# A one-core hybrid layer: the experts' first u and v are loaded and split during the gate stage, row sums come one step later, and adds of y move behind other readers of PSUM

## The chip, the cores and the metric

The kernel runs on one core of a Trainium2 chip. The metric is the device time of one execution in microseconds; the median of three runs of the kernel before is 3334.67 us (3320.79 to 3336.86).

## What is computed

One layer: a mixer (three kinds of attention on 1,024 tokens of 1,024 features), then PEER, a layer of 16,384 one-neuron experts. The last part is what the change touches, cut to its core:

```
q = (hb @ w_q).reshape(T, 8, 2, 128)                       # 8 heads, two half queries
s = einsum('thpd,pkd->thpk', q, keys)                      # 128 keys a half
top_s, top_i = top_k(s, 16); best_s, pos = top_k(all 256 sums of the two halves, 16)
idx = key_a * 128 + key_b of the best 16;  g = softmax(best_s)
act = gelu(einsum('thkd,td->thk', u[idx], hb))             # 128 experts a token
y   = einsum('thkd->td', g * act * v[idx])
out = x + gate2 * y
```

All is float32. Large products are done as three products of high and low parts (hi*hi, hi*lo, lo*hi).

## The kernel before, in words

After the mixer come three blocks: `route`, `gate_matrix` and `experts`. The 1,024 tokens are two halves. For the first 512 (tiles 0 to 3, "A") the chosen rows are gathered; for the second 512 (tiles 4 to 7, "B") all experts are computed densely.

- **Dots of A, ahead.** `Ahead` (L1366) computes the activations gelu(u x) of all 128 chunks of 128 experts for the A tokens while `route` and `gate_matrix` run: a chunk of u (512 KB) is loaded by SP, ScalarE makes its high part (`split_high`), GpSimd the low part (`split_low`), TensorE does 24 matmuls (`dots`), ScalarE the gelu, and SP stores the result to `act_scratch` in DRAM.
- **Gates of B.** `gate_matrix` builds for the B tokens the dense matrix of gates from one-hot products and stores it in 8 pieces of 4,096 KB to `gate_scratch`, issued by ScalarE. Its SP block ends by waiting for all stores; then the next block begins on all engines.
- **Experts.** `experts` (L1905) runs 64 steps of two chunks c = 0, 1 of 128 experts. In each, for the B tokens: u of the chunk is split into high (ScalarE) and low (VectorE), TensorE does 24 matmuls for the dots in PSUM (`dot_products`), ScalarE the gelu, VectorE multiplies with the gates (`weigh`) and makes the low part of the weights (`low_weights`), and in the next step TensorE multiplies the weights with v (`outputs`, 24 matmuls per c). Half of the outputs stays in PSUM over all steps (`held`), the other half (`y`) is added to `total` in SBUF by VectorE each step (`add`, four a step).
- **Rows of A.** Beside this GpSimd issues 16 indirect DMAs a step: 8 elements (`element`, L2009: the activation of one pick per token of a tile) and 8 rows (`row`, L2014: 128 rows of v, 512 KB, to one of 8 slots of `ring`). VectorE weights the picks (`weigh_picks`) and adds each row times its weight to `total` (`add_row`, L2152). GpSimd fetches a row for step s+1 once the row of step s has left the slot (`row_added`).

Each engine works through its instructions in the written order, so the place of each in VectorE's list is what decides. For one c of a step the order before is:

```
add_row(s, 4 * c, opening)
low_v(s, b, c)
add_row(s, 4 * c + 1, opening)
weigh(s, c)
low_u(n + 2, c, False)
low_weights(s, b, c)
add(s - 1, 2 * c, first)
add_row(s, 4 * c + 2, opening)
add_row(s, 4 * c + 3, opening)
add(s - 1, 2 * c + 1, first)
```

After 64 steps VectorE adds the last y, multiplies each of the 8 token tiles with `gate2` and adds x1 (`finish`), and SP stores it.

Of the kernel before, what the change touches and what calls it, by code (L numbers as in the profile page):

```python
# [13 lines left out]
F32 = mybir.dt.float32  # L14
F32R = mybir.dt.float32r
# [1350 lines left out]
class Ahead:  # L1366
# [3 lines left out]
    def __init__(self, nc, ctx, d, hi, lo, acts, tag, base):  # L1370
        sb, ps, sem = allocators(nc, ctx)
        self.nc, self.src, self.hi, self.lo, self.acts, self.base = nc, d["peer_u"], hi, lo, acts, base
        self.u = sb(tag + "u", [P, 2, KD, P])
        self.uhi = sb(tag + "uhi", [P, 2, KD, P], F32R)
        self.ulo = sb(tag + "ulo", [P, 2, KD, P], F32R)
# [63 lines left out]

class RouteInputs:  # L1440
# [14 lines left out]
def route(nc, k, d, hi, lo, first_T, second_T, gate_T, sparse, acts, inputs):  # L1455
# [9 lines left out]
    with ExitStack() as ctx:  # L1465
        sb, ps, sem = allocators(nc, ctx)
        first_key, second_key, gate = (sb(n, [P, NT, P]) for n in ("first_key", "second_key", "pick_gate"))
        ahead = Ahead(nc, ctx, d, hi[0], lo[0], acts, "ra_", 0)
# [298 lines left out]
def gate_matrix(nc, d, hi, lo, first_T, second_T, gate_T, scratch, acts):  # L1767
# [3 lines left out]
    with ExitStack() as ctx:  # L1771
        sb, ps, sem = allocators(nc, ctx)
        ahead = Ahead(nc, ctx, d, hi, lo, acts, "ga_", ROUTED)
# [10 lines left out]
        assert STEPS == NB // 2  # L1784

# [10 lines left out]
        with nc.Block() as block:  # L1796
            @block.sync
            def _(sp):
# [47 lines left out]
            def _(act):  # L1846
# [26 lines left out]
                block_pair(STEPS - 1, False, True)  # L1873

            @block.vector
            def _(dve):
# [21 lines left out]
                with dve.Fori(1, STEPS) as step:  # L1898
                    block_pair(step, False)

# [4 lines left out]
def experts(nc, k, d, hi, lo, total, scratch, acts, sparse, x1, result):  # L1905
# [10 lines left out]
    with ExitStack() as ctx:  # L1916
        sb, ps, sem = allocators(nc, ctx)
        u = sb("ex_u", [P, 2, KD, P])
        uhi = sb("ex_uhi", [P, 2, KD, P], F32R)
        ulo = sb("ex_ulo", [P, 2, KD, P], F32R)  # L1920
        v = sb("ex_v", [P, 2, D])
# [10 lines left out]
        u_in, v_in, g_in, pick_in = ([sem(f"ex_{n}_in{c}") for c in range(2)] for n in ("u", "v", "g", "pick"))  # L1932
# [3 lines left out]
        uhi_ready, ulo_ready, vhi_ready, vlo_ready, dots_ready, gelu_ready, weighted, whi_ready, wlo_ready, \  # L1936
            y_ready, y_added, held_ready, zeroed, pick_weighted, row_added = map(sem, (
                "ex_uhi_ready", "ex_ulo_ready", "ex_vhi_ready", "ex_vlo_ready", "ex_dots_ready",
# [6 lines left out]

        def one(a, n, pattern):
            return a[n] if isinstance(n, int) else a[bass.ds(n, 1)].rearrange(pattern)
# [12 lines left out]
        with nc.Block() as block:  # L1960
            @block.sync
            def _(sp):
                def load_u(n, c):
# [385 lines left out]
```

## Time and profile before

| | |
|---|---|
| median of the runs | 3334.67 us (3320.79 to 3336.86) |
| the profiled execution: own time / span | 3342.92 / 3341.1 us |
| TensorE busy | 3136.2 us (94%) |
| VectorE busy | 2363.6 us (71%) |
| GpSimd (POOL) busy | 1673.7 us (50%) |
| ScalarE busy | 1015.7 us (30%) |
| mean granted clock of TensorE | 0.963 of full speed |
| DMA | 645.75 MB, 193 GB/s over the span |

How to read it: the span is from the first to the last instruction of the profiled execution. Busy times of POOL include its indirect DMA issues, those of the other engines exclude their DMA issues. In the rows below PE is TensorE, DVE VectorE, ACT ScalarE, SP the engine that issues most loads; a row names the line of the kernel, the operation and its tiles (output <- inputs). Two operations in a row on one engine overlap by some 0.08 us in the rows, so the distance of two starts is the duration that counts. Up to 1836 us the mixer, routing and gate stages run, after it the expert stage.

### The profile page before, as it was taken

The page shows a single profiled execution, that of the slowest core. Times are in us where ns is not written, and L with a number is a line of the kernel's source. Part 1 is how long each engine was busy: PE and PEld are TensorE (multiplying, and loading weights), DVE is VectorE, ACT ScalarE, POOL GpSimd, SP SyncE. Part 2 cuts the span into 40 slices and gives each one's busy share as a digit, 9 for nine tenths or more (in the row PEclk, how much of TensorE's full clock was granted, in tenths as well). Part 3 has the DMA queues.
Part 4 walks back from the last instruction along what each step waited for, and adds up shares of the span by engine and source line. Part 5 has one row for each costly group of instructions (what it writes and reads, how often), then busy time and mean ns, then how long its engine had stood idle before and what let it go on. Part 6 is the DMA issues. An engine that isn't in the chain of part 4 may idle for free. (4 is left out here: it accounts for less than half of the span.)

```text
span 3341.1 us, 44529 instructions
## 1 busy us (share of the span) xinstructions
PE 3136.2 (94%) x14956; PEld 2541.8 (76%) x14956; DVE 2363.6 (71%) x4287; ACT 1015.7 (30%) x1182; POOL 1673.7 (50%) x1329
## 2 busy tenths in 40 slices
PE   6999588997999999999998799999999999999997
PEld 3889465686888887888887677777777877777776
DVE  4612465463688888666664688888888888888888
ACT  2110134432333323444444222222222222222221
POOL 2000224413433323333332777777777777777774
PEclk7999678998999999999999899999999999999999
DMA  5610000022332323445444898898898999999897
GB/s 208 212 64 26 10 14 26 1 91 91 111 107 88 107 79 123 159 160 214 163 163 189 272 298 298 288 297 287 293 299 302 304 301 300 298 306 300 292 306 283
DMA packets 325786, 645.75 MB, mean 193 GB/s; under 512 B 169264, under 2 KB 170560, under 8 KB 322752
## 3 DMA queue, kind: packets, MB, share of 16 engines
q1 hardware_dynamic: 233280, 338.08, 31.7%
q0 software_dynamic: 91264, 272.96, 23.1%
q10 hardware_dynamic: 1152, 33.55, 2.4%
q8 instruction: 51, 0.84, 0.1%
q14 instruction: 39, 0.32, 0.0%
HBM read 568.98 MB, written 75.50 MB: 193 GB/s over the span
## 5 line engine op out<-in xcount | busy, mean ns | idle before, releaser
L2152 DVE SCALAR_TENSOR_TENSOR total<-ex_ring,ex_pick,total 128x1024 f32<-128x1024 f32 x512 | 650.7, 1291 | 225.9 <-DMA ex_ring<-peer_v_dram,sp_row 217.6
L2009 POOL DMA_INDIRECT ex_pick<-act_scratch,sp_place x512 | 576.7, 1126 | 175.7 <-issue 155.7
L2014 POOL DMA_INDIRECT ex_ring<-peer_v_dram,sp_row x512 | 578.1, 1129 | 156.1 <-issue 129.9
L2042 PE MATMUL ex_dots<-h_hi_b,ex_uhi 128*128 128x512 f32 x1024 | 401.3, 392 | 23.7 <-ACT ex_uhi L2084 14.4
L2042 PE MATMUL ex_dots<-h_lo_b,ex_uhi 128*128 128x512 f32 x1024 | 400.7, 391 | 0.0
L1891 DVE TENSOR_SCALAR gm_b_hot<-gm_iota,second_T,gate_T 128x128 f32<-128x128 f32 x512 | 257.7, 571 | 170.1 <-PE gm_prod L1835 167.4
L2101 ACT ACTIVATE ex_whi<-ex_dots 128x512 fp32r<-128x512 f32 x128 | 76.8, 600 | 925.0 <-DVE ex_dots L2132 925.0
L1415 POOL TENSOR_TENSOR ga_ulo<-ga_u,ga_uhi 128x1024 fp32r<-128x1024 f32 x72 | 173.2, 2407 | 341.8 <-ACT ga_uhi L1409 341.6
L2045 PE MATMUL ex_dots<-h_hi_b,ex_ulo 128*128 128x512 f32 x1024 | 252.8, 389 | 0.0
L2052 PE MATMUL ex_y<-ex_vhi,ex_whi 128*128 128x512 f32 x512 | 216.3, 422 | 33.7 <-DVE total L2123 27.9
L2042 PEld LDWEIGHTS ex_dots<-h_hi_b,ex_uhi 128*128 128x128 f32 x1024 | 193.9, 189 | 64.9 <-ACT ex_uhi L2084 14.9
L1415 POOL TENSOR_TENSOR ra_ulo<-ra_u,ra_uhi 128x1024 fp32r<-128x1024 f32 x56 | 139.1, 2485 | 205.6 <-ACT ra_uhi L1409 205.6
L1425 PE MATMUL ga_dots<-h_hi_a,ga_uhi 128*128 128x512 f32 x576 | 229.9, 399 | 0.0
L2042 PEld LDWEIGHTS ex_dots<-h_lo_b,ex_uhi 128*128 128x128 f32 x1024 | 193.8, 189 | 40.3
L1425 PE MATMUL ga_dots<-h_lo_a,ga_uhi 128*128 128x512 f32 x576 | 224.5, 390 | 0.0
L2045 PEld LDWEIGHTS ex_dots<-h_hi_b,ex_ulo 128*128 128x128 f32 x1024 | 192.2, 188 | 39.9
L2052 PE MATMUL ex_y<-ex_vlo,ex_whi 128*128 128x512 f32 x512 | 201.1, 393 | 0.0
L2052 PE MATMUL ex_y<-ex_vhi,ex_wlo 128*128 128x512 f32 x512 | 200.8, 392 | 0.0
L2052 PE MATMUL ex_held<-ex_vhi,ex_whi 128*128 128x512 f32 x512 | 200.0, 391 | 0.0
L2052 PE MATMUL ex_held<-ex_vlo,ex_whi 128*128 128x512 f32 x512 | 199.5, 390 | 0.0
L2052 PE MATMUL ex_held<-ex_vhi,ex_wlo 128*128 128x512 f32 x512 | 199.3, 389 | 0.0
L2052 PEld LDWEIGHTS ex_y<-ex_vhi,ex_whi 128*128 128x128 f32 x512 | 96.1, 188 | 108.6 <-DVE total L2123 83.9
(302 smaller groups left out, 6758.4 us busy)
## 6 DMA issues: line engine op xcount, KB each, us to landing
ex_u<-peer_u_dram SPq DMA_DIRECT2D x128, 512.0 KB, 5.5
ex_v<-peer_v_dram SPq DMA_DIRECT2D x128, 512.0 KB, 8.0
ga_u<-peer_u_dram SPq DMA_DIRECT2D x72, 512.0 KB, 3.6
gate_scratch<-gm_out ACTq DMA_DIRECT2D x8, 4096.0 KB, 11.8
ex_g<-gate_scratch SPq DMA_DIRECT2D x128, 256.0 KB, 6.5
ra_u<-peer_u_dram SPq DMA_DIRECT2D x56, 512.0 KB, 3.6
act_scratch<-ga_act SPq DMA_DIRECT2D x72, 256.0 KB, 2.1
w_in_raw<-w_ada_dram SPq DMA_DIRECT2D x64, 256.0 KB, 3.7
```

The lines of the kernel that those rows point to most:

```text
L1415: eng.tensor_tensor(self.ulo[:, c], self.u[:, c], self.uhi[:, c].bitcast(F32), ALU.subtract).then_inc(self.ulo_ready, 1)
L1425: self.nc.tensor.matmul(self.ps[:, c], self.uhi[:, c, kk], b[:, kk], start=kk == 0 and b is self.hi, stop=False)
L1891: last = nc.vector.tensor_scalar(b_hot[:, g % 2, t], iota[:], second_T[:, token], gate_T[:, token], ALU.is_equal, ALU.mult)
L2009: nc.gpsimd.indirect_dma_start(weights[:, i:i + 1], None, places, bass.IndirectOffsetOnAxis(ap=picks[:, i:i + 1], axis=0)).then_inc(pick_i ...
L2014: nc.gpsimd.indirect_dma_start(ring[:, i], None, rows, bass.IndirectOffsetOnAxis(ap=which[:, RING * s + i:RING * s + i + 1], axis=0)).then ...
L2042: nc.tensor.matmul(dots[:, c], uhi[:, c, kk], b[:, kk], start=kk == 0 and b is hi, stop=False)
L2045: mm = nc.tensor.matmul(dots[:, c], ulo[:, c, kk], hi[:, kk], start=False, stop=kk == KD - 1)
L2052: mm = nc.tensor.matmul(dst, w[:, b, c, t * P:(t + 1) * P], x[:, b, c, half * HALF:(half + 1) * HALF], start=opens and c == 0 and w is whi ...
L2101: nc.scalar.activation(whi[:, b, c], dots[:, c], ACT.Copy).then_inc(whi_ready, 1)
L2152: nc.vector.scalar_tensor_tensor(total[:, t], ring[:, i], weights[:, bass.ds(PER * s + i, 1)], total[:, t], ALU.mult, ALU.add).then_inc(ro ...
```

## The change

1. One object `ExpertInputs` now holds the buffers of u and v and their semaphores for all three blocks. In the last gate step SP loads u of experts' chunks 0 and 1, then v of both, ScalarE and VectorE split u, and SP loads u of chunks 2 and 3, all before the block ends. The waits for the stores go from SP's end of `gate_matrix` to the start of `experts`: on SP (before the loads of g), on ScalarE and on GpSimd (before the first element).
2. GpSimd issues the 8 elements of step 0, then its 8 rows, instead of by turns.
3. VectorE weights picks and adds rows of step s-1 in step s; the eight of the last step follow the loop.
4. VectorE adds y directly behind `weigh` and behind `low_weights`, instead of ahead of and behind the last two row adds.
5. The last four adds of y stand between the last row adds instead of between the finished tiles.

```
class ExpertInputs:
    ...
    def load_u(self, sp, n, c): ...
    def load_v(self, sp, n, c): ...
    def high_u(self, act, c, turn):
        act.wait_ge(self.u_in[c], 16 * turn + 16)
        self.nc.scalar.activation(self.uhi[:, c], self.u[:, c], ACT.Copy).then_inc(self.uhi_ready, 1)
    def low_u(self, dve, n, c):
        dve.wait_ge(self.uhi_ready, n + 1)
        self.nc.vector.scalar_tensor_tensor(self.ulo[:, c], self.uhi[:, c].bitcast(F32), -1.0, self.u[:, c],
                                            ALU.mult, ALU.add).then_inc(self.ulo_ready, 1)
    def stores_done(self, eng):
        for stored, count in self.stores:
            eng.wait_ge(stored, count)
```

```diff
 gate_matrix, SP
                     for c in range(PER_STEP):
-                        ahead.load_and_store(sp, PER_STEP * step + c, c % 2, not last or c < PER_STEP - 2)
+                        n, more = PER_STEP * step + c, not last or c < PER_STEP - 2
+                        if not more:
+                            sp.wait_ge(ahead.ulo_ready, n + 1)
+                            stream.load_u(sp, c % 2, c % 2)
+                        ahead.load_and_store(sp, n, c % 2, more)
...
-                ahead.stores_done(sp, STEPS * PER_STEP)
-                for b in range(2):
-                    sp.wait_ge(stored[b], 16 * STEPS)
+                for c in range(2):
+                    stream.load_v(sp, c, c)
+                for c in range(2):
+                    sp.wait_ge(stream.ulo_ready, c + 1)
+                    stream.load_u(sp, 2 + c, c)
 gate_matrix, ScalarE and VectorE, at their ends
+                for c in range(2):
+                    act.wait_ge(ahead.dots_ready, COUNT - 1 + c)
+                    stream.high_u(act, c, 0)
...
+                for c in range(2):
+                    dve.wait_ge(ahead.dots_ready, COUNT - 1 + c)
+                    stream.low_u(dve, c, c)
 experts, SP
+                stream.stores_done(sp)
                 for c in range(2):
-                    load_u(c, c)
-                for c in range(2):
-                    load_v(c, c)
                     load_g(c, c)
-                for c in range(2):
-                    sp.wait_ge(ulo_ready, c + 1)
-                    load_u(2 + c, c)
 experts, GpSimd
+                stream.stores_done(pool)
                 for i in range(PER):
                     element(0, i)
+                for i in range(PER):
                     row(0, i)
 experts, VectorE
-                    weigh_picks(s, b, s // 2)
+                    if not opening:
+                        weigh_picks(s - 1, 1 - b, s // 2 - 1 + b)
                     for c in range(2):
                         n = 2 * s + c
-                        add_row(s, 4 * c, opening)
+                        if not opening:
+                            add_row(s - 1, 4 * c, first)
...
                         low_v(s, b, c)
-                        add_row(s, 4 * c + 1, opening)
+                        if not opening:
+                            add_row(s - 1, 4 * c + 1, first)
                         weigh(s, c)
+                        if not opening:
+                            add(s - 1, 2 * c, first)
                         if not last or n + 2 < CH:
-                            low_u(n + 2, c, False)
+                            low_u(n + 2, c)
                         low_weights(s, b, c)
                         if not opening:
-                            add(s - 1, 2 * c, first)
-                        add_row(s, 4 * c + 2, opening)
-                        add_row(s, 4 * c + 3, opening)
-                        if not opening:
                             add(s - 1, 2 * c + 1, first)
+                            add_row(s - 1, 4 * c + 2, first)
+                            add_row(s - 1, 4 * c + 3, first)
...
+                weigh_picks(ST - 1, 1, ST // 2 - 1)
+                for i in range(PER):
+                    add_row(ST - 1, i, False)
+                    if i % 2:
+                        add(ST - 1, i // 2, False)
...
                 for t in range(NT):
-                    if t < HELD:
-                        add(ST - 1, t, False)
```

VectorE in the first half (c = 0) of step 62, before; the steps in the loop have the same operations. `ex_pick` is the weighting of picks, `total<-ex_ring` a row add, `ex_vlo` and `ex_ulo` the low parts of v and u, `ex_dots` the weighting with gates, `ex_wlo` the low part of the weights, `total<-total,ex_y` an add of y:

```order
L2141 TENSOR_TENSOR ex_pick<-ex_pick,sp_gate 128x8
L2152 SCALAR_TENSOR_TENSOR total<-ex_ring,ex_pick,total 128x1024
L2109 SCALAR_TENSOR_TENSOR ex_vlo<-ex_vhi,ex_v 128x1024
L2152 SCALAR_TENSOR_TENSOR total<-ex_ring,ex_pick,total 128x1024
L2132 SCALAR_TENSOR_TENSOR ex_dots<-ex_g,ex_dots 128x512
L2109 SCALAR_TENSOR_TENSOR ex_ulo<-ex_uhi,ex_u 128x1024
L2109 SCALAR_TENSOR_TENSOR ex_wlo<-ex_whi,ex_dots 128x512
L2123 TENSOR_TENSOR total<-total,ex_y 128x512
L2152 SCALAR_TENSOR_TENSOR total<-ex_ring,ex_pick,total 128x1024 x2
L2123 TENSOR_TENSOR total<-total,ex_y 128x512
```

The same place now (the x3 takes in the first row add of the second half):

```order
L2176 TENSOR_TENSOR ex_pick<-ex_pick,sp_gate 128x8
L2187 SCALAR_TENSOR_TENSOR total<-ex_ring,ex_pick,total 128x1024
L2146 SCALAR_TENSOR_TENSOR ex_vlo<-ex_vhi,px_v 128x1024
L2187 SCALAR_TENSOR_TENSOR total<-ex_ring,ex_pick,total 128x1024
L2167 SCALAR_TENSOR_TENSOR ex_dots<-ex_g,ex_dots 128x512
L2158 TENSOR_TENSOR total<-total,ex_y 128x512
L1472 SCALAR_TENSOR_TENSOR px_ulo<-px_uhi,px_u 128x1024
L2146 SCALAR_TENSOR_TENSOR ex_wlo<-ex_whi,ex_dots 128x512
L2158 TENSOR_TENSOR total<-total,ex_y 128x512
L2187 SCALAR_TENSOR_TENSOR total<-ex_ring,ex_pick,total 128x1024 x3
```

The first add of y stands between the gate weighting and the split of u, the second directly behind the low part of the weights, and the row adds follow one another.

VectorE at the end, before, from the last split of v to the second finished tile:

```order
L2109 SCALAR_TENSOR_TENSOR ex_vlo<-ex_vhi,ex_v 128x1024
L2152 SCALAR_TENSOR_TENSOR total<-ex_ring,ex_pick,total 128x1024
L2132 SCALAR_TENSOR_TENSOR ex_dots<-ex_g,ex_dots 128x512
L2109 SCALAR_TENSOR_TENSOR ex_wlo<-ex_whi,ex_dots 128x512
L2123 TENSOR_TENSOR total<-total,ex_y 128x512
L2152 SCALAR_TENSOR_TENSOR total<-ex_ring,ex_pick,total 128x1024 x2
L2123 TENSOR_TENSOR total<-total,ex_y 128x512 x2
L2189 TENSOR_TENSOR total<-total,gate 128x1024
L2193 TENSOR_TENSOR total<-total,ex_ring 128x1024
L2123 TENSOR_TENSOR total<-total,ex_y 128x512
L2189 TENSOR_TENSOR total<-total,gate 128x1024
```

and now, from the last weighting of picks:

```order
L2176 TENSOR_TENSOR ex_pick<-ex_pick,sp_gate 128x8
L2187 SCALAR_TENSOR_TENSOR total<-ex_ring,ex_pick,total 128x1024 x2
L2158 TENSOR_TENSOR total<-total,ex_y 128x512
L2187 SCALAR_TENSOR_TENSOR total<-ex_ring,ex_pick,total 128x1024 x2
L2158 TENSOR_TENSOR total<-total,ex_y 128x512
L2187 SCALAR_TENSOR_TENSOR total<-ex_ring,ex_pick,total 128x1024 x2
L2158 TENSOR_TENSOR total<-total,ex_y 128x512
L2187 SCALAR_TENSOR_TENSOR total<-ex_ring,ex_pick,total 128x1024 x2
L2158 TENSOR_TENSOR total<-total,ex_y 128x512
L2224 TENSOR_TENSOR total<-total,gate 128x1024
L2228 TENSOR_TENSOR total<-total,ex_ring 128x1024
```

The row adds of the last step follow all its other work, and the adds of y have left the finishing sequence.

## Rows read from the trace of the kernel before

**Rows 1.** Page, section 5: POOL's two groups; busy us, mean ns, idle before

```profile
L2009 POOL DMA_INDIRECT ex_pick<-act_scratch,sp_place x512 | 576.7, 1126 | 175.7 <-issue 155.7
L2014 POOL DMA_INDIRECT ex_ring<-peer_v_dram,sp_row x512 | 578.1, 1129 | 156.1 <-issue 129.9
```

**Rows 2.** Waits of POOL, 1836 to 3303 us: total us, times, longest us

```profile
POOL ex_pick L2009 <- issue: 155.7, 511, 0.3
...
POOL ex_ring L2014 <- DVE total L2152: 26.2, 86, 0.3
```

**Rows 3.** Timeline of PE, 3280 to 3322 us: start, duration, operation

```profile
3293.96 1.98 PE L2045 MATMUL ex_dots<-h_hi_b,ex_ulo 128*128 128x512 f32 x8
...
3304.84 1.98 PE L2045 MATMUL ex_dots<-h_hi_b,ex_ulo 128*128 128x512 f32 x8
```

**Rows 4.** Timeline of POOL, one step: start, duration, operation, idle before

```profile
2618.80 1.66 POOL L2014 DMA_INDIRECT ex_ring<-peer_v_dram,sp_row  x1 [0.30 <-issue]
...
2622.01 0.95 POOL L2014 DMA_INDIRECT ex_ring<-peer_v_dram,sp_row  x1 [0.30 <-DVE total L2152]
2623.26 1.31 POOL L2009 DMA_INDIRECT ex_pick<-act_scratch,sp_place  x1 [0.30 <-issue]
2624.88 0.94 POOL L2014 DMA_INDIRECT ex_ring<-peer_v_dram,sp_row  x1 [0.30 <-issue]
2626.12 0.94 POOL L2009 DMA_INDIRECT ex_pick<-act_scratch,sp_place  x1 [0.31 <-issue]
...
2628.62 1.38 POOL L2009 DMA_INDIRECT ex_pick<-act_scratch,sp_place  x1 [0.30 <-issue]
...
2632.80 0.95 POOL L2014 DMA_INDIRECT ex_ring<-peer_v_dram,sp_row  x1 [0.30 <-issue]
```

**Rows 5.** Timeline of DVE, the same step

```profile
2619.56 1.22 DVE L2109 SCALAR_TENSOR_TENSOR ex_vlo<-ex_vhi,ex_v 128x1024 fp32r<-128x1024 f32 x1
...
2621.94 0.68 DVE L2132 SCALAR_TENSOR_TENSOR ex_dots<-ex_g,ex_dots 128x512 f32<-128x512 f32 x1
2622.54 1.21 DVE L2109 SCALAR_TENSOR_TENSOR ex_ulo<-ex_uhi,ex_u 128x1024 fp32r<-128x1024 f32 x1
2623.67 0.68 DVE L2109 SCALAR_TENSOR_TENSOR ex_wlo<-ex_whi,ex_dots 128x512 fp32r<-128x512 f32 x1
...
2624.87 2.51 DVE L2152 SCALAR_TENSOR_TENSOR total<-ex_ring,ex_pick,total 128x1024 f32<-128x1024 f32 x2
...
2633.30 1.28 DVE L2152 SCALAR_TENSOR_TENSOR total<-ex_ring,ex_pick,total 128x1024 f32<-128x1024 f32 x1 [2.99 <-DMA ex_ring<-peer_v_dram,sp_row]
```

**Rows 6.** Timelines of POOL and PE, 1800 to 1910 us, the stage's start

```profile
1836.02 1.01 POOL L2009 DMA_INDIRECT ex_pick<-act_scratch,sp_place  x1 [20.02 <-POOLq L1796]
...
1840.85 0.80 PE L2042 MATMUL ex_dots<-h_hi_b,ex_uhi 128*128 128x512 f32 x1 [14.43 <-ACT ex_uhi L2084]
```

**Rows 7.** DMA issues of two tiles, 1820 to 1836 us, and their landing

```profile
L1863 ACTq DMA_DIRECT2D gate_scratch<-gm_out x1: 348/348/348, 1823.0 to 1823.0; - x1
...
DMA to landing us min/median/max: 11.3/11.3/11.3
...
L1399 SPq DMA_DIRECT2D act_scratch<-ga_act x2: 333/338/344, 1819.8 to 1827.1; - x2
...
DMA to landing us min/median/max: 2.0/4.8/7.7
```

**Rows 8.** Timelines of POOL and DVE, 1800 to 1910 us

```profile
1867.45 1.97 POOL L2009 DMA_INDIRECT ex_pick<-act_scratch,sp_place  x1 [0.31 <-issue]
...
1867.38 1.22 DVE L2109 SCALAR_TENSOR_TENSOR ex_vlo<-ex_vhi,ex_v 128x1024 fp32r<-128x1024 f32 x1
```

**Rows 9.** Timelines of POOL and DVE, 3255 to 3341 us, the end

```profile
3301.71 0.94 POOL L2014 DMA_INDIRECT ex_ring<-peer_v_dram,sp_row  x1 [0.30 <-issue]
...
3297.82 0.15 DVE L2141 TENSOR_TENSOR ex_pick<-ex_pick,sp_gate 128x8 f32<-128x8 f32 x1
...
3316.97 1.22 DVE L2189 TENSOR_TENSOR total<-total,gate 128x1024 f32<-128x1024 f32 x1
```

More of the change, by code:

```diff
@@ L1437, in gelu, with __init__, sb, load_u @@
         self.nc.scalar.activation(self.out[:, c], self.ps[:, c], ACT.Gelu).then_inc(self.gelu_ready, 1)
+class ExpertInputs:
+    def __init__(self, nc, ctx, d):
+        sem = allocators(nc, ctx)[2]
+        def sb(name, shape, dt=F32):
+            return ctx.enter_context(nc.sbuf_tensor(name, shape, dt, side="right", align_bytes=LINE if dt is F32R else 32))
+        self.nc, self.d = nc, d
+        self.u = sb("px_u", [P, 2, KD, P])
+        self.uhi = sb("px_uhi", [P, 2, KD, P], F32R)
+        self.ulo = sb("px_ulo", [P, 2, KD, P], F32R)
+        self.v = sb("px_v", [P, 2, D])
+        self.u_in, self.v_in = ([sem(f"px_{n}_in{c}") for c in range(2)] for n in ("u", "v"))
+        self.uhi_ready, self.ulo_ready = sem("px_uhi_ready"), sem("px_ulo_ready")
+        self.stores = []
+    def load_u(self, sp, n, c):
+        src = self.d["peer_u"][n] if isinstance(n, int) else \
+            self.d["peer_u"][bass.ds(n, 1)].rearrange("a p k i -> (a p) k i")
+        sp.dma_start(self.u[:, c], src).then_inc(self.u_in[c], 16)
+    def load_v(self, sp, n, c):
+        src = self.d["peer_v"][n] if isinstance(n, int) else \
+            self.d["peer_v"][bass.ds(n, 1)].rearrange("a i d -> (a i) d")
+        sp.dma_start(self.v[:, c], src).then_inc(self.v_in[c], 16)
+    def high_u(self, act, c, turn):
+        act.wait_ge(self.u_in[c], 16 * turn + 16)
+        self.nc.scalar.activation(self.uhi[:, c], self.u[:, c], ACT.Copy).then_inc(self.uhi_ready, 1)
+    def low_u(self, dve, n, c):
[5 more added lines that the diff above has]
+            eng.wait_ge(stored, count)
 class RouteInputs:
@@ L1784, in gate_matrix @@
         assert STEPS == NB // 2
+        COUNT = STEPS * PER_STEP
+        stream.stores = [(a, 16 * COUNT // 2) for a in ahead.stored] + [(a, 16 * STEPS) for a in stored]
         slots = [c * GPI // PER_STEP for c in range(PER_STEP)]
@@ L1931, in experts @@
         y = ps("ex_y", [P, 2, HALF])
-        u_in, v_in, g_in, pick_in = ([sem(f"ex_{n}_in{c}") for c in range(2)] for n in ("u", "v", "g", "pick"))
+        g_in, pick_in = ([sem(f"ex_{n}_in{c}") for c in range(2)] for n in ("g", "pick"))
+        u_in, v_in, uhi_ready, ulo_ready = stream.u_in, stream.v_in, stream.uhi_ready, stream.ulo_ready
         row_in = [sem(f"ex_row_in{i}") for i in range(RING)]
@@ L2079, in _, with split_u @@
             def _(act):
-                def split_u(n, c, turn, first):
-                    act.wait_ge(u_in[c], 16 * turn + 16)
-                    if not first:
-                        act.wait_ge(dots_ready, n - 1)
-                    nc.scalar.activation(uhi[:, c], u[:, c], ACT.Copy).then_inc(uhi_ready, 1)
-                for c in range(2):
-                    split_u(c, c, 0, True)
+                def split_u(n, c, turn):
+                    act.wait_ge(dots_ready, n - 1)
+                    stream.high_u(act, c, turn)
+                stream.stores_done(act)
                 def stage(s, b, first, last):
@@ L2109, in low_part, with low_u @@
                     return nc.vector.scalar_tensor_tensor(dst, high.bitcast(F32), -1.0, full, ALU.mult, ALU.add)
[L2111 to L2115 removed]
+                def low_u(n, c):
+                    dve.wait_ge(dots_ready, n - 1)
+                    stream.low_u(dve, n, c)
                 def add(s, n, first):
@@ L2269, in trunk @@
         sparse = Sparse(nc, ctx)
+        stream = ExpertInputs(nc, ctx, d)
         picked = picks.enter_context(ExitStack())
```

50 lines of the change are left out of this document (16 added, 34 removed).

## The prediction

> **What bounds the kernel now.** I read the page first, then the waits by engine, and then the timelines of POOL and VectorE (DVE in the rows) side by side over one step of the expert stage, because the share of busy time misleads here. TensorE (PE) is busy nearly all the time, yet it does not set the pace of the expert stage, which takes 1,500 of the 3,341 us. Its two half steps of 48 matmuls lie 10.88 us apart when nothing holds it [rows 3], so 21.8 us a step. POOL issues 16 indirect DMAs a step, eight elements and eight rows. They take 1.126 and 1.129 us on average [rows 1], and the 0.3 us ahead of each is put down to "issue" or to VectorE, at the longest 0.3 us [rows 2]: POOL has not waited for anybody once. From its first issue at 1836.02 [rows 6] to the last one, which ends at 3302.65 [rows 9], are 1466.6 us for 1,024 instructions, 22.9 us a step. So POOL sets the pace, and VectorE waits for the rows that it fetches (2.99 us before the row add at 2633.30 [rows 5]).
>
> Why does an issue take 1.13 us, when most take 0.94? Rows 4 and 5 show it. The POOL instruction of 2623.26 begins while VectorE splits u (2622.54 to 2623.67) and takes 1.31; that of 2618.80 begins during a row add that ends at 2619.56, where the next row of the timeline begins, and takes 1.66. Each of them ends 0.90 us after the end of the VectorE operation in whose time it began (2623.67 + 0.90 = 2624.57). The operations that hold POOL back are those with two operands in SBUF: row adds, the low parts of u and v. Those with an operand in PSUM (gate weights times dots, low part of the weights, add of y) do not: the issue of 2622.01 begins in the gate weighting of 2621.94 and takes 0.95. One more thing matters: an issue that begins only 0.01 or 0.06 us after such an operation started is free (2624.88 beside the row add of 2624.87, and 2626.12 beside the second of this pair, begun 1.20 us later) [rows 4, 5]. Sixteen free issues of 0.945 with 0.305 between them would take 20.0 us a step; the stage's 22.9 therefore hold 2.9 us of this holding.
>
> The Trainium skill ("SBUF — State Buffer", section "Who interferes with whom") states the same selection: a DVE instruction with at most one SBUF input leaves GpSimd alone, one with two contends with a GpSimd instruction that reads SBUF. It adds that whichever starts first has the pair for its whole length and the other blocks fully. For VectorE the trace differs: the row add of 2633.30 takes 1.28 although the issue of 2632.80 runs until 2633.75, and two such adds in a row take 2.51 where POOL issues as well [rows 4, 5]. By the page's sentence VectorE would wait behind issues as well, in both orders alike, VectorE would set the pace, and only the tail's -8.6 below would be left of the change: 3326. I go by the trace.
>
> **The change part by part.** The times below are against the profiled execution (span 3341.1, its own time 3342.92); the median of the runs is 3334.67, 8.25 lower, and I carry this difference along.
>
> *Early u and v.* TensorE starts at 1840.85 after 14.43 us of idling [rows 6]. With u0 and u1 split while the last gate chunk ends, it can start after the splits, about 1831. But POOL reads act_scratch and so must wait for the stores. The store of 4096 KB is issued at 1823.0 and lands 11.3 us later, that of the last activations, issued at 1827.1, lands 7.7 us later, both by 1834.8 [rows 7]. The new loads of v and u are issued from about 1827.5 on and queue up behind the same large store; 256 KB took 7.7 us there and 2.0 before it [rows 7], so what comes second waits and does not delay the store (bounds: 0, and for 2 MB sharing evenly, at the 370 GB/s of 4096 KB in 11.3 us, +6; I take 0). POOL starts when the stores have landed instead of one barrier later: **-0.8 us**. The 9 us of TensorE are hidden by POOL and count nothing; if POOL weren't the bound they would count in full. POOL's first 24 issues now fall beside VectorE at work on steps 0 and 1 instead of idling; four more held ones at about 0.5: **+2** (0 to 4).
>
> *Row sums one step later.* In the steady stage the position of the row adds among the other work is the same, with rows of one step earlier; they are fetched in the same order with the same distance. Nothing changes as long as POOL is the bound. At the end it pays. Before, 19.15 us pass from the last weighting of picks (3297.82) to the first multiply with the gate (3316.97) [rows 9]. After, this stretch holds eight row adds at 1.20, four adds of y at 0.60 and the weighting, 0.28: 12.3. Three more adds of y (1.8) leave the finishing sequence. TensorE's last 48 matmuls (10.9 us) begin a step earlier and fit beside it. **-8.6 us** (0 to -9).
>
> *Adds of y behind PSUM readers.* This touches POOL's holding, 2.9 us a step times 61, so it can be worth more than all the rest. I walk a half step from the start w of the gate weighting, in the usual case that the row add before it held an issue (which ends at w+0.90; the next starts at w+1.21, then every 1.25). Before: split of u from 0.60 to 1.73 holds that issue (0.48), the next two fall 0.01 and 0.06 into the row adds and are free, the fourth falls into the row add ahead of the split of v: 0.43 (the issue of 2628.62, 1.38), or 0.71 in the half step with the weighting of picks (that of 2618.80, 1.66) [rows 4]. Sum per step 2 x 0.48 + 0.43 + 0.71 = 2.10. After: 0 gates, 0.60 add, 1.20 split of u, 2.33 low weights, 2.93 add, 3.53 and 4.72 row adds, 5.92 third row add (6.20 with the pick weighting before it), 7.12 split of v (7.40). POOL at 1.21 (0.01 into the split: free), 2.46 (free), 3.71: 0.18 into the row add, held until 4.72, 0.97 lost. Then 5.93 (0.01: free) and 7.18 (0.06: free); with picks 7.18 falls into the row add that ends at 7.40: 0.17. Sum 0.97 + 0.97 + 0.17 = 2.11. The remaining 0.8 of the 2.9 belongs to the row adds at random phase ahead of w and stays. The half steps in which no issue is held there lose more than before (held in the split of u until 2.33, about 1.0 for 0.4), partly made up elsewhere; I put 0.1 a step, **+6 us** over 61 steps. Bounds: holding nothing, down to TensorE's pace, (22.9 - 21.8) x 61 = -69; one more hold of 1.03 a step, +63. I stay near zero because the walk is made of durations that repeat to 0.01 us.
>
> Sum: -0.8 + 2 - 8.6 + 6 = -1.4, so 3341.5 for such an execution and **3333 us** as a median.
>
> **The rivals.**
> 1. *Holding falls away, TensorE takes over.* Two stretches of 1.2 us without a two-SBUF operation now exist where 0.60 stood. If POOL's phase settles so that the issue at 3.71 comes 0.2 earlier, 1.9 us a step are gained, more than the 1.1 to TensorE's pace: 3333 - 69 - 6 = 3258; a share of it, 3290 to 3315, if it does so in some half steps. Against it: the 0.18 is twenty times the scatter of the intervals. Chance 0.17.
> 2. *The early start counts.* If POOL's schedule has slack that the rows don't show, TensorE's 9.6 us and the tail's 8.6 come off: 3334.67 - 18 = 3316. Against it stand the waits of at most 0.3 [rows 2]. Chance 0.10.
> 3. *Slower: the issue 0.06 into the split of v is caught.* It is free by one row, but the issue of 1867.45, 0.07 after the split of v of 1867.38, took 1.97 [rows 8]. If it is caught each step, 1.03 x 61 = +63: 3396. It decides from 0.07 us on. A milder form: the third row add comes 0.6 earlier than before and meets rows that have not landed, which shifts POOL's phase and costs 0.3 to 0.5 a step: 3351 to 3364. Chance 0.23 together.
>
> **The numbers.** A measurement of this kernel tells about 0.5% (17 us) from no change. My case, 0.50, lies within 3318 to 3350. Faster by more: 0.27 (rival 1, rival 2). Slower by more: 0.23. The range 3292 to 3370 leaves out the full forms of rivals 1 and 3, about 0.1 each. Inside my own case alone 3322 to 3346.
>
> **What would show it.** First POOL issue near 1835.2, first expert matmul near 1831 to 1833; POOL never idle over 0.3; mean issue 1.13 (below 1.07: rival 1; 1.19: rival 3); issues of about 1.9 us in the first row add behind the add of y, none beside the split of u; from the last pick weighting to the first gate multiply 12 us. I am wrong if POOL waits for row adds, or if the mean issue moves by more than 0.02.

## The result, and the profile after

The changed kernel takes **3413.30 us** (median of 4 runs, 3395.72 to 3419.31) against 3332.94 us for the kernel before in the same comparison. The ratio is 1.0239, 95% interval 1.019 to 1.0287: slower by 80 us. The forecast was 3333, range 3292 to 3370, so it was wrong, and outside its range. The profiled execution of the changed kernel has a span of 3417.5 us, 76.4 more than the 3341.1 of before. POOL's two groups, from section 5 of the page after, answer to [rows 1]; the waits of POOL from 1842 to 3384 us (total us, times, longest us) to [rows 2]:

```profile
L2047 POOL DMA_INDIRECT ex_pick<-act_scratch,sp_place x512 | 634.4, 1239 | 176.5 <-issue 155.8
L2052 POOL DMA_INDIRECT ex_ring<-peer_v_dram,sp_row x512 | 596.3, 1165 | 156.0 <-issue 150.5
```

```profile
POOL ex_pick L2047 <- issue: 155.8, 511, 0.3
POOL ex_ring L2052 <- issue: 150.5, 494, 0.3
POOL ex_ring L2052 <- DVE total L2187: 5.5, 18, 0.3
```

POOL still waits for nobody. The same 1,024 issues take 1,202 ns on average, not 1,128: 75.8 us in all. The timelines of POOL and VectorE after, around the first issue and the end, show the other differences:

```profile
1840.86 1.01 POOL L2047 DMA_INDIRECT ex_pick<-act_scratch,sp_place  x1 [20.75 <-DMA act_scratch<-ga_act]
...
3381.79 1.48 POOL L2052 DMA_INDIRECT ex_ring<-peer_v_dram,sp_row  x1 [0.30 <-issue]
...
3376.48 0.20 DVE L2176 TENSOR_TENSOR ex_pick<-ex_pick,sp_gate 128x8 f32<-128x8 f32 x1
...
3393.34 1.28 DVE L2187 SCALAR_TENSOR_TENSOR total<-ex_ring,ex_pick,total 128x1024 f32<-128x1024 f32 x1 [1.17 <-DMA ex_ring<-peer_v_dram,sp_row]
...
3395.14 1.22 DVE L2224 TENSOR_TENSOR total<-total,gate 128x1024 f32<-128x1024 f32 x1
```

The 76.4 us split exactly. POOL begins at 1840.86, 4.8 later than before [rows 6]. From there to the end of its last issue (3383.27) are 1542.4 us, against 1466.6: **+75.8**. From that end to the end of the kernel are 34.2, against 38.4 [rows 9]: -4.2. So everything that matters is in the length of POOL's issues.

One half step of the changed kernel and the start of the next, POOL first and VectorE below, show where they are held:

```profile
2610.09 1.91 POOL L2047 DMA_INDIRECT ex_pick<-act_scratch,sp_place  x1 [0.30 <-issue]
2612.30 0.94 POOL L2052 DMA_INDIRECT ex_ring<-peer_v_dram,sp_row  x1 [0.30 <-issue]
2613.55 0.94 POOL L2047 DMA_INDIRECT ex_pick<-act_scratch,sp_place  x1 [0.30 <-issue]
2614.80 0.95 POOL L2052 DMA_INDIRECT ex_ring<-peer_v_dram,sp_row  x1 [0.30 <-issue]
2616.05 1.96 POOL L2047 DMA_INDIRECT ex_pick<-act_scratch,sp_place  x1 [0.30 <-issue]
...
2622.70 0.94 POOL L2047 DMA_INDIRECT ex_pick<-act_scratch,sp_place  x1 [0.30 <-issue]
...
2625.20 1.97 POOL L2047 DMA_INDIRECT ex_pick<-act_scratch,sp_place  x1 [0.30 <-issue]
```

```profile
2609.97 1.21 DVE L1472 SCALAR_TENSOR_TENSOR px_ulo<-px_uhi,px_u 128x1024 fp32r<-128x1024 f32 x1
2611.11 0.67 DVE L2146 SCALAR_TENSOR_TENSOR ex_wlo<-ex_whi,ex_dots 128x512 fp32r<-128x512 f32 x1
2611.70 0.67 DVE L2158 TENSOR_TENSOR total<-total,ex_y 128x512 f32<-128x512 f32 x1
2612.30 3.75 DVE L2187 SCALAR_TENSOR_TENSOR total<-ex_ring,ex_pick,total 128x1024 f32<-128x1024 f32 x3
2615.97 1.21 DVE L2146 SCALAR_TENSOR_TENSOR ex_vlo<-ex_vhi,px_v 128x1024 fp32r<-128x1024 f32 x1
...
2622.68 1.27 DVE L1472 SCALAR_TENSOR_TENSOR px_ulo<-px_uhi,px_u 128x1024 fp32r<-128x1024 f32 x1
2623.87 0.67 DVE L2146 SCALAR_TENSOR_TENSOR ex_wlo<-ex_whi,ex_dots 128x512 fp32r<-128x512 f32 x1
...
2625.07 2.47 DVE L2187 SCALAR_TENSOR_TENSOR total<-ex_ring,ex_pick,total 128x1024 f32<-128x1024 f32 x2
```

The issue of 2610.09 begins 0.12 us into the split of u and takes 1.91. After it POOL and VectorE run in step. Issues start at 2612.30, 2613.55 and 2614.80, the row adds 1.20 to 1.24 apart from 2612.30 on, so an issue falls 0.00, then 0.05, then 0.07 us after the start of an operation; all three are free. The next falls 0.08 us into the split of v (2616.05 against 2615.97) and takes 1.96. The issue of 2622.70, 0.02 us into the split of u, is free; the one 0.13 us into the row adds of 2625.07 takes 1.97.

I grouped every issue of the stage over 1.0 us by the VectorE operation in whose time it begins (times, and the sum of what they take beyond 0.945):

| | in row adds | in splits of u | in splits of v | sum |
|---|---|---|---|---|
| before | 212, 127.3 us | 127, 58.1 | 1, 1.0 | 187 |
| after | 246, 169.1 us | 34, 33.2 | 60, 60.9 | 263 |

(The sums are over all 1,024 issues.) The trade is plain: 25 us won in the splits of u, 60 lost in the splits of v, 42 lost in row adds. Of these, only the loss in the splits of v is wholly outside the forecast (see the section on the prediction).

The edges can be read from the same rows. After, all 58 issues that begin 0.04 to 0.07 us into a split of v are held. The 92 at 0.00 or 0.01 into a split of u are free, and all 33 at 0.04 to 0.13 are held. Of those that begin 0.04 to 0.08 us into a row add, all 61 are free; the 105 at 0.09 to 0.14 are all held. **A split catches an issue some 0.05 us earlier than a row add does.** The prediction took the edge of row adds for both.

Is it the kind of operation, or what stands ahead of it? The fourteenth run has a split of u directly behind a split of v:

```profile
2602.32 1.97 POOL L2047 DMA_INDIRECT ex_pick<-act_scratch,sp_place  x1 [0.30 <-issue]
```

```profile
2602.25 1.22 DVE L1472 SCALAR_TENSOR_TENSOR px_ulo<-px_uhi,px_u 128x1024 fp32r<-128x1024 f32 x1
```

All 119 issues that begin 0.06 or 0.07 us into a split so placed are held. Of the issues that begin 0.06 or 0.07 us into a row add directly behind a split of v, 281 of 284 are free (all sixteen traces). So with the same operation ahead, the kind decides. The edge of a row add is less sharp than the changed kernel shows it: 3 issues at 0.07 are held, and in other traces some at 0.09 and 0.10 are free.

### The profile page after: what moved, and what is told of

It reads as the page before. It is cut to its first block, busy times and chain, and to the rows that moved or that the text cites. A ratio compares the mean times of both kernels' runs of the same rounds, so it can differ in the third digit from the quotient of the medians.

```text
span 3417.5 us, 44386 instructions
## 1 busy us (share of the span) xinstructions
PE 3144.3 (92%) x14956; PEld 2570.3 (75%) x14956; DVE 2366.3 (69%) x4287; ACT 1010.5 (30%) x1182; POOL 1746.6 (51%) x1329
## 4 chain that ended last, share of the span: by engine, by line
POOL 32%; PE 15%; issue 9%; DMA 3%; DVE 2%; DVEq 0%; POOLq 0%; ACT 0%
POOL ex_pick L2047 16%; POOL ex_ring L2052 15%; PE ga_dots L1423 8%; PE ga_dots L1427 4%; PE gm_prod L1883 3%; DMA ex_ring<-peer_v_dram,sp_row 3%; DVE total L2187 1%; DVE total L2158 0%; DMA act_scratch<-ga_act 0%; DVE ex_wlo L2146 0%; DVE total L2224 0%; DVE ex_dots L2167 0%; DVE ex_vlo L2146 0%; DVE total L2221 0%; DVE gm_b_hot L1942 0%
## 5 line engine op out<-in xcount | busy, mean ns | idle before, releaser
L1413 POOL TENSOR_TENSOR px_ulo<-px_u,px_uhi 128x1024 fp32r<-128x1024 f32 x128 | 310.0, 2423 | 549.5 <-ACT px_uhi L1407 549.3
L2082 PE MATMUL ex_dots<-h_hi_b,px_uhi 128*128 128x512 f32 x1024 | 399.4, 390 | 7.6 <-PEq L1838 7.6
L2082 PE MATMUL ex_dots<-h_lo_b,px_uhi 128*128 128x512 f32 x1024 | 399.1, 390 | 0.0
L2085 PE MATMUL ex_dots<-h_hi_b,px_ulo 128*128 128x512 f32 x1024 | 252.8, 389 | 0.0
L1423 PE MATMUL ga_dots<-h_hi_a,px_uhi 128*128 128x512 f32 x576 | 230.4, 400 | 0.0
L2082 PEld LDWEIGHTS ex_dots<-h_hi_b,px_uhi 128*128 128x128 f32 x1024 | 192.7, 188 | 48.1 <-issue 8.0
L1423 PE MATMUL ga_dots<-h_lo_a,px_uhi 128*128 128x512 f32 x576 | 224.7, 390 | 0.0
L2082 PEld LDWEIGHTS ex_dots<-h_lo_b,px_uhi 128*128 128x128 f32 x1024 | 192.8, 188 | 40.0
L2085 PEld LDWEIGHTS ex_dots<-h_hi_b,px_ulo 128*128 128x128 f32 x1024 | 192.2, 188 | 39.9
L1423 PE MATMUL ra_dots<-h_hi_a,px_uhi 128*128 128x512 f32 x448 | 175.7, 392 | 0.0
## 6 DMA issues: line engine op xcount, KB each, us to landing
w_ada_half<-w_ada_dram SPq DMA_DIRECT2D x4, 2048.0 KB, 13.9
```

Of the source, the lines that this page charges most:

```text
L1413: eng.tensor_tensor(self.ulo[:, c], self.u[:, c], self.uhi[:, c].bitcast(F32), ALU.subtract).then_inc(self.ulo_ready, 1)
L1423: self.nc.tensor.matmul(self.ps[:, c], self.uhi[:, c, kk], b[:, kk], start=kk == 0 and b is self.hi, stop=False)
L2082: nc.tensor.matmul(dots[:, c], uhi[:, c, kk], b[:, kk], start=kk == 0 and b is hi, stop=False)
L2085: mm = nc.tensor.matmul(dots[:, c], ulo[:, c, kk], hi[:, kk], start=False, stop=kk == KD - 1)
```

## The experiments

Theory A: the moved adds of y shift the operations on VectorE so that issues of POOL land in splits and row adds where they are held; nothing else in the change costs anything. Theory B: the early loads or the later row sums cost it. Times are medians; a ratio with an interval rests on several runs of both kernels. Experiments 4, 5, 6, 13 and 14 are one run each. "Before" is the kernel before on the same chip.

**1. The adds of y put back.**

```diff
                         weigh(s, c)
-                        if not opening:
-                            add(s - 1, 2 * c, first)
...
                         low_weights(s, b, c)
                         if not opening:
-                            add(s - 1, 2 * c + 1, first)
+                            add(s - 1, 2 * c, first)
                             add_row(s - 1, 4 * c + 2, first)
                             add_row(s - 1, 4 * c + 3, first)
+                            add(s - 1, 2 * c + 1, first)
```

> The changed kernel with its adds of y put back (one behind the low part of the weights, one behind the two row adds); early u and v and the later row sums stay. Theory A (the moved adds bring issues of POOL 0.04 to 0.07 us into a split of u or v, where they are held until 0.90 us after its end, although the same offset into a row add is free): mean issue back to 1.13 us, POOL's stage back to about 1467 us from 1542, time 3413 - 75 = 3338, and some 4 us less by the shorter end: 3325 to 3345. Theory B (the early loads or the later row sums cost it): stays at 3395 to 3420.

Measured: 3334.92 us, ratio to before 1.0015 (1.0003 to 1.0027). Mean issue 1.124, POOL's stage 1462.4 us, 3 issues in splits of v. This is what Theory A gives, with the early loads and the later row sums in place.

**2. The kernel before with only the adds of y moved** (the same edit the other way).

> The kernel before with nothing but the two adds of y moved behind the gate weighting and behind the low part of the weights. Theory A: most of the loss is there, mean issue 1.19 or more, 3390 to 3415. Theory B: no loss, 3325 to 3345.

Measured: 3412.12 us against 3332.17, ratio 1.0265 (1.0234 to 1.0295). Its page has the changed kernel's numbers within 2 ns:

```profile
L2009 POOL DMA_INDIRECT ex_pick<-act_scratch,sp_place x512 | 634.2, 1239 | 175.8 <-issue 155.8
L2014 POOL DMA_INDIRECT ex_ring<-peer_v_dram,sp_row x512 | 595.3, 1163 | 156.0 <-issue 149.0
```

The adds of y alone make the whole loss; with the first run this is shown from both sides.

**3. Split of v ahead of the first row add.**

```diff
-                        if not opening:
-                            add_row(s - 1, 4 * c, first)
...
                         low_v(s, b, c)
                         if not opening:
+                            add_row(s - 1, 4 * c, first)
                             add_row(s - 1, 4 * c + 1, first)
```

> The changed kernel with one exchange in VectorE's list: the split of v stands ahead of the first row add of its half step, not behind it. The two operations are equally long. Theory A (what counts is whether a split or a row add begins 0.04 to 0.07 us ahead of an issue): the issue at 7.18 us of the half step now falls 0.06 us into a row add and is free, that at 5.93 falls 0.01 us into the split and is free; mean issue 1.12 to 1.14, time 3325 to 3350. Theory C (the number of two-SBUF operations in a row, or VectorE's load, costs it, whichever they are): no change, 3395 to 3420.

Measured: 3397.0 us, ratio 1.0194 (1.0162 to 1.0226). My expectation by Theory A failed, and the time is the one that Theory C of the expectation gives (the series of two-SBUF operations costs it, whichever they are). POOL and VectorE of this kernel show what happens:

```profile
2600.42 1.97 POOL L2047 DMA_INDIRECT ex_pick<-act_scratch,sp_place  x1 [0.31 <-issue]
2602.69 2.03 POOL L2052 DMA_INDIRECT ex_ring<-peer_v_dram,sp_row  x1 [0.30 <-issue]
```

```profile
2600.30 2.47 DVE L2187 SCALAR_TENSOR_TENSOR total<-ex_ring,ex_pick,total 128x1024 f32<-128x1024 f32 x2
2602.69 1.21 DVE L2146 SCALAR_TENSOR_TENSOR ex_vlo<-ex_vhi,px_v 128x1024 fp32r<-128x1024 f32 x1
```

Behind a row add the split catches even an issue that begins with it: 45 of the 49 issues that begin less than 0.01 us into a split of v behind a row add are held in this kernel. This edge is not fixed: in the second, eleventh and twelfth runs four issues at 0.01 and one at 0.02 behind a row add are free. Behind the weighting of picks 18 issues that begin with a split of v or 0.01 ahead of it are free, and behind an add of y the splits of u let issues at 0.00 and 0.01 through. The rows show a second thing as well. An issue held in one row add ends 0.90 us after it, and the next begins 0.30 later: 1.20 after that end, which is the length of a row add. So POOL does not meet the operations at random; after such a hold it is put onto the start of an operation, and then walks on by 0.05 (1.25 against 1.20) or less, since an issue just behind the start of a row add makes this longer. Theory C falls with the seventh order below: it has four two-SBUF operations in a row too, and takes 3261 us.

**4. Early loads alone, order of VectorE as before.**

> The changed kernel with the whole order of VectorE in the expert stage, and its end, put back to that of before; the early loads and splits of u and v, the moved waits for the stores and the order of POOL's first issues stay. Theory A: close to the kernel before, 3325 to 3345; first POOL issue about 13.7 us behind the last store of activations against 13.0 before, so no gain either. Theory B (early loads cost it): over 3380.

Measured: 3333.92 us in one run, mean issue 1.116. The last gate store is issued at 1823.86 and the first POOL issue at 1837.55, 13.7 later (the expectation names the store of activations, and means this one). Theory B falls for the early loads.

**5. Later row sums alone; 6. fewer elements; 7, 8. two new orders.** These shared a chip on which the kernel before took 3586 us (3579 to 3603), and where TensorE stood idle before some of its matmuls with nothing but "issue" ahead of them (125 us between 2000 and 3300 us of the fifth run, where 94 of some 5,800 matmuls start 0.7 us behind the one before, instead of the usual 0.23). Times from that chip say nothing on the theories, except where the kernel ran undisturbed, as the sixth did. The fifth, seventh and eighth were run again.

> The kernel before with the rows summed one step later and the last adds of y between the last row adds (parts 3 and 5 alone). Theory A (only the moved adds cost anything): mean issue 1.12 to 1.14, 3322 to 3345. Rival (a row a step late costs something by itself): over 3360.

3573.35 beside 3586, mean issue 1.119. Again, as e13:

> The kernel before with parts 3 and 5 alone once more (its first run shared the disturbed chip): 3322 to 3345 beside 3320 to 3345 of the kernel before; the end from POOL's last issue to the last operation of VectorE 34 us against 38.4. Rival: over 3360.

3328.06 us in one run, before 3338.51; mean issue 1.126, 33.8 us from POOL's last issue to the end. The fourth experiment and this one are one run each, but the first has both parts in it and takes 3334.92: neither early loads nor later row sums cost anything.

> The changed kernel with one element fetched per step in place of eight (seven of eight weights of the first 512 tokens are left at 0, VectorE and TensorE do all their work). POOL then issues 9 times a step. If POOL's issues set the pace of 24.1 us a step (1542.4 us for 64), the stage falls to TensorE's 21.8 a step: 3413 - 2.3 x 64 = 3265, within 10. If VectorE's order itself or the landing of the rows made it slow, it stays above 3380.

Measured: 3258.45 us (one run), a step of 21.76. The kernel leaves out seven of eight weights, so it is a measurement and no version to use. POOL now waits for VectorE (waits of POOL, 1900 to 3200 us):

```profile
POOL ex_ring L2054 <- DVE total L2190: 497.0, 125, 5.7
```

With the same order on VectorE and 9 issues a step in place of 16, the stage falls to TensorE's pace. Some of the difference may come from the smaller traffic; together with the runs that follow it shows that POOL's issues set the pace, and that nothing is wrong with the new order as such.

For the seventh and eighth I walked POOL through every order of the ten operations of a half step, with the edges read so far (row adds from 0.09, splits from 0.03, behind a two-SBUF operation from 0.00) and durations from the rows, and took two of those that it gave TensorE's pace.

(The order of the seventh; the conditions `if not opening` and the old lines are left out.)

```diff
 order 7
+                        low_v(s, b, c)
+                        add_row(s - 1, 4 * c, first)
+                        add_row(s - 1, 4 * c + 1, first)
+                        add_row(s - 1, 4 * c + 2, first)
+                        add(s - 1, 2 * c, first)
+                        low_u(n + 2, c)
+                        add_row(s - 1, 4 * c + 3, first)
+                        add(s - 1, 2 * c + 1, first)
+                        weigh(s, c)
+                        low_weights(s, b, c)
```

> The changed kernel with another order of VectorE per half step: split of v, three row adds, add of y, split of u, fourth row add, add of y, gate weighting, low part of the weights. Chosen by walking POOL through it: an issue held in an operation resumes 1.20 us after that operation's end, which is one row add (1.20) later, so issues fall onto starts of operations; splits hold at 0.00 (behind a row add) or from 0.03 to 0.04 on, row adds from 0.09 on. Here one issue a half step is held in the split of u (0.8) and one at its end by 0.1. Theory A: mean issue 1.06, step 21.8 (TensorE's pace), POOL no longer the bound, 3255 to 3285. Rival D (moved operations cost TensorE or VectorE waits that the walk leaves out): over 3310.

> As the kernel before it, another order found by the same walk: both adds of y, split of v, two row adds, gate weighting, low part of the weights, split of u, two row adds. Theory A: one issue held in the split of v (0.5), one in the split of u (0.3), mean issue 1.06, 3255 to 3285. Rival D: over 3310. If only one of the two orders keeps to the walk, the edges for the splits are set too late or too early in it.

On the disturbed chip 3615 and 3559 us beside 3586 (ratios 1.0084 and 0.9918), with mean issues of 1.047 and 1.103: there the new orders gain little or nothing. Again, on a chip where the kernel before took 3341.04:

> The first new order once more, since in the call before this one the kernel before itself took 3586 us in place of 3332 and TensorE got its matmuls 0.7 us apart in many places. Where the kernel before takes 3320 to 3340 again: Theory A, mean issue 1.05 as seen there (1.144 for rows, 0.950 for elements), POOL not the bound, step 21.8, 3255 to 3285. Rival D (the order costs TensorE waits): over 3310. Where the kernel before takes 3580 again: 3600 to 3630 again, and nothing is told apart.

> The second new order once more, for the same reason. Theory A: 3255 to 3285 beside a kernel before of 3320 to 3340. Its issues took 1.193 (rows) and 1.013 (elements) in the disturbed call, 1.10 on average, which puts POOL at (1.10 + 0.305) x 16 = 22.5 a step: if that holds here too, 3300 to 3315.

Measured: **3260.72 us, ratio 0.9766 (0.9723 to 0.981)**, and 3265.36, ratio 0.9784 (0.9743 to 0.9825). Mean issues 1.061 and 1.056, a step of 21.74 and 21.76. In the windows of the first, 2200 to 2500 and 2500 to 2800 us (PE, PEld, DVE, ACT, POOL busy, clock, DMA share, GB/s), TensorE shows no pause:

```profile
2200.00:2500.00 300.00, 300.00 (x1326) 248.56 (x1325) 271.90 (x291) 85.05 (x110) 232.75 (x221) 1.00 0.93 314
2500.00:2800.00 300.00, 300.00 (x1325) 248.60 (x1324) 269.05 (x290) 85.06 (x110) 232.96 (x221) 1.00 0.93 312
```

This version beats both kernels. POOL does not pause in it either (its idle time is never over 0.31): 16 issues at TensorE's 21.75 a step leave (21.75 / 16) - 0.305 = 1.054 for each, so a mean issue of 1.06 tests the walk no further than the time does. Where the holds fall, the walk did not get right: about 0.8 us a half step in the split of u were expected, and 0.48 were found there and 0.29 in the split of v. Once TensorE sets the pace, the tail comes near the forecast: from the last weighting of picks to the first multiply are 12.2 us in this order (rows of VectorE) and 13.9 in the other:

```profile
3232.39 0.16 DVE L2176 TENSOR_TENSOR ex_pick<-ex_pick,sp_gate 128x8 f32<-128x8 f32 x1
...
3244.62 1.22 DVE L2226 TENSOR_TENSOR total<-total,gate 128x1024 f32<-128x1024 f32 x1
```

**11, 12. Each add of y moved alone; 14. an order that the walk gives as bad.** In e11 the second add stands behind the two row adds again; in e12 both stand behind the low part of the weights; in e14 the split of u comes directly behind the split of v.

> The changed kernel with only the first add of y moved (behind the gate weighting); the second stands behind the two row adds as before. Theory A by the walk with the edges read so far (splits caught from 0.03 us, behind a row add from 0.00; row adds from 0.09): the add of y between the second and the third row add of the series keeps the split of v from falling 0.05 us ahead of an issue: hardly any issue is held in the split of v (under 15), mean issue 1.13 to 1.155, 3335 to 3365. If the first add is what costs: 3395 to 3420.

> The changed kernel with both adds of y behind the low part of the weights: the split of u directly behind the gate weighting as before, the three row adds and the split of v in one series as in the change. Theory A: some 60 issues held in the split of v for 60 us as in the change, and the 126 short ones in the split of u as before; mean issue 1.18 to 1.20, 3385 to 3415. If the series of two-SBUF operations does no harm without the shift of the split of u: 3325 to 3345.

> A test of the walk in the other direction, with an order that it gives as worse than the change: row add, split of v, split of u, row add, gate weighting, add of y, low part of the weights, add of y, two row adds. Theory A: about 105 issues held in the split of u for about 1.0 us each and 22 in the split of v, mean issue 1.23 to 1.26, 3440 to 3480. If the walk only fits what it was made from: near 3413 or below.

| | time (before 3338.51) | mean issue | in row adds | splits of u | splits of v |
|---|---|---|---|---|---|
| e11 | 3436.42, ratio 1.0289 (1.0261 to 1.0317) | 1.226 | 364, 253.5 us | 31, 30.0 | 5, 4.6 |
| e12 | 3410.95, ratio 1.0214 (1.0188 to 1.0241) | 1.202 | 272, 150.3 | 125, 56.4 | 55, 55.7 |
| e14 | 3336.9 (one run) | 1.124 | 125, 54.1 | 122, 123.4 | 7, 7.0 |

e12 came as expected: with the split of u left in its old place, the series of three row adds and the split of v is enough for the loss. e11 and e14 did not. In e11 the splits of v are clear of issues as forecast (5), yet it is the slowest. A form of holding appears there that the walk did not know:

```profile
2598.76 2.57 POOL L2047 DMA_INDIRECT ex_pick<-act_scratch,sp_place  x1 [0.30 <-issue]
```

```profile
2598.11 1.27 DVE L2187 SCALAR_TENSOR_TENSOR total<-ex_ring,ex_pick,total 128x1024 f32<-128x1024 f32 x1
2599.30 1.21 DVE L2146 SCALAR_TENSOR_TENSOR ex_vlo<-ex_vhi,px_v 128x1024 fp32r<-128x1024 f32 x1
```

The issue begins in a row add and ends 0.90 after the end of the split of v behind it (2600.43 + 0.90 = 2601.33): it was held through both. There are 54 such issues, 88 us; all begin 0.53 to 0.55 us ahead of the split (5 others there were held in the row add alone). In the kernel before there is one. It takes a split behind the row add: in e12, at the same distance ahead of another row add, none of 122 issues is held through both. In e14 the splits hold about as many issues as expected (122 and 7, for 105 and 22), but the row adds hold 54 us, where the expected mean issue of 1.23 to 1.26 asks for 165 to 195; that the sum is near that of before is chance. So the walk had the time right on two good orders and a bad one (e12), and wrong on two (e11 and e14). It is a search tool whose finds must be measured, not a forecast.

## Why the prediction was wrong, point by point

- **What bounds the kernel: right.** POOL's 1,024 issues set the pace before and after (waits of at most 0.3; the sixth run; the two new orders end at 21.8 a step, the figure worked out from [rows 3]).
- **Adds of y, +6: the step that failed**, at "Then 5.93 (0.01: free) and 7.18 (0.06: free)". The issue does arrive where the walk had it, 0.05 to 0.07 us behind the start of the split of v (58 issues). The 0.06 was called free by a row add of [rows 5], an operation of another kind, while the one row on a split, the issue of [rows 8] held at 0.07, pointed the other way and was put into a rival. Measured: +75.8 us for the whole term. Of the stated sum, the first hold of 0.97 in the row add is there (2625.20, 1.02 lost). The walk had 1.14 us a step in row adds before and 2.11 after (+59 us over 61 steps) and 0.96 in splits of u before and none after (-59); the trace has +42 and -25, so these two came out near +17, where +6 was put. The rest, 60 us, is the split of v, which the walk had at nothing. "None beside the split of u" failed for 34 issues (33 us).
- **The size of rival 3** was 63, "it decides from 0.07 us on". 60 issues are held in the split of v, about one a step: 61 us, so this part was sized well. It gave 3396 and had about 0.1; the time is 3413. In the splits the holding decides from some 0.03 us on, not 0.07. The row that pointed to it stands, in the kernel before, behind three row adds in a row, the very place that the change makes the rule.
- **Early u and v, -0.8: measured +0.7.** From the issue of the last gate store to the first POOL issue are 13.0 us in all four traces with the old start [rows 6, 7] and 13.7 in the eleven with the new one (the sixth run, which first clears the weights, left out). The large store lands after 12.0 us, not 11.3: it does share with the new loads, of which I had taken the lower bound. What POOL waits for is the last store of activations (the row of 1840.86): it now lands 8.8 us after its issue, not 7.7, which costs 1.1, while POOL starts 0.9 behind that landing in place of 1.25, which gives back 0.4. The first expert matmul came 2.7 us ahead of POOL's first issue; before it came 4.8 behind. The rest of the 4.8 us later start is the scatter of the stages ahead: that store is issued between 1814.5 and 1827.2 us over the sixteen traces, whatever the kernel.
- **Early steps, +2:** not separable. It is part of the 75.8: the first 24 issues take 7.1 us beyond 0.945 each in the changed kernel and 5.0 before, but 3.2 to 4.9 in the first, third and fourth runs, which start alike.
- **Row sums a step later, -8.6: measured -4.2** in the change, and -4.6 in e13 alone (the old end varies: 36.1 us from POOL's last issue in e2, 38.4 before, 39.9 in e4). The working held for VectorE, but not for what it waits for: with POOL as the bound the last four rows land 6.2 to 10.0 us after the end of their issues, and the eight row adds wait 6.0 us for rows (1.17 of them at 3393.34). From the last weighting of picks to the first multiply are 18.7 us, not 12.3. With TensorE as the bound they are 12.2 and 13.9.
- **Rival 1, 3258 by TensorE's pace,** was a good price for another order: 3260.72 for the seventh. It did not come by itself.
- **The page's sentence.** The Trainium skill ("SBUF — State Buffer", section "SBUF: two separate sides") says that whichever starts first has the shared ports for its whole length and the other blocks fully. That a later issue is blocked by an operation in progress, the trace bears out (2610.09). That who starts first decides, it does not quite: the issues of 2622.70, 0.02 us into the split of u, and of 2613.55, 0.05 into a row add, are free. And it does not bear out a block of VectorE for an issue's length: that split takes until the next operation at 2623.87, 1.19 against 1.14, so it lost 0.05 us and not the issue's 0.94. The 3326 by that sentence did not come.

What stays open: why a split catches an issue earlier than a row add, both being the same instruction (the row add has a third operand in SBUF, its weight; I did not test that); why a few issues at the same distance ahead of a split are held through the row add alone (5 of 59 in e11); why the row adds of e14 hold so little; and what starved TensorE on the other chip.

## What to carry to other kernels

When two engines hold each other up, find the length of a held step and of a free one, and compare them with the lengths of the other engine's operations. Here 0.90 + 0.30 = 1.20 equals a row add and 1.25 is 0.05 more, so offsets don't average out but lock, and one operation moved by 0.6 us or an order changed at the same work is worth from -80 to +100 us, on a chip where POOL is the bound. Take an edge of hundredths from rows of the very kind of operation that it is applied to, and if a single row contradicts, give it the larger chance. A good order can be found by walking all of them, and is worth only what a run confirms.

## What the runs showed of the hardware that I had not expected

- The edge from which VectorE holds an indirect DMA issue depends on the operation and on what stands ahead of it: 0.09 us for a row add in the changed kernel (0.07 to 0.10 over all traces), between 0.02 and 0.03 for a split of u behind an add of y, 0.00 to 0.02 for a split of v behind a row add.
- An issue can be held through two adjacent operations (2.57 us in place of 0.94), seen where the second is a split.
- The reverse effect is small and has the same shift between the two kinds. The split of u takes 1.14 us, but 1.18 if a free issue begins with it, 1.19 at 0.01 and 1.22 at 0.04; the row add takes 1.20 up to an issue at 0.01, then 1.23 at 0.05 and 1.26 at 0.08 (means over the sixteen traces).
- On one chip the kernel before took 3586 us instead of 3332. The fifth run has nearly the usual issue lengths on POOL there (1.119), but gaps ahead of matmuls for which its rows show no cause; with 9 issues a step in place of 16 the changed kernel ran there in 3258 without any such gap.
